# FFN: the raw turned tokens are put together by GpSimd, tile by tile, instead of by VectorE in two adds

## The reference, cut to what matters

```python
def rms_norm(x, g):
    y = xf * lax.rsqrt(jnp.mean(xf * xf, axis=-1, keepdims=True) + RMS_EPS)
    return (y * g).astype(x.dtype)

def swiglu(h, w_in, w_out):
    gate, up = jnp.split(h @ w_in, 2, axis=-1)
    return (jax.nn.silu(gate) * up) @ w_out

def macaron_half(x, g_pre, g_post, w_in, w_out):
    return x + FFN_RES_SCALE * rms_norm(swiglu(rms_norm(x, g_pre), w_in, w_out), g_post)
```

## Time and profile before

| | |
|---|---|
| median of 3 runs | 2520.59 us (2514.84 to 2521.19) |
| span of the profiled execution, first to last instruction | 2515.4 us |
| time of the profiled execution beside its span | not given |
| TensorE matmul busy | 2438.8 us, 97% |
| TensorE weight load busy | 2219.3 us, 88% |
| VectorE busy | 1502.0 us, 60% |
| ScalarE busy | 1078.2 us, 43% |
| GpSimd busy | 138.5 us, 6% |
| mean granted TensorE clock | 0.997 |

### The profile page before, as it was taken

How to read it: one execution, slowest core, us unless ns; L and a number is a source line. 1 busy time by engine, 2 the same in 40 slices (tenths; PEclk the granted TensorE clock), 3 DMA queues, 4 the chain that set the end, 5 groups by cost and what they waited for, 6 DMA issues and landing times. The chain is left out here.

```text
span 2515.4 us, 46249 instructions
## 1 busy us (share of the span) xinstructions
PE 2438.8 (97%) x18529; PEld 2219.3 (88%) x18529; DVE 1502.0 (60%) x2111; ACT 1078.2 (43%) x1873; POOL 138.5 (6%) x150
## 2 busy tenths in 40 slices
PE   8999999999988989999999999999999999999998
PEld 7998998899667877998999899899989779988997
DVE  7754764423546866873675687267462478735754
ACT  5542543322645654452353445245352444523542
POOL 0000001000203421000000100000010010000001
PEclk9999999999999999999999999999999999999999
DMA  4222324222480004322223332223423132322332
GB/s 134 84 86 74 84 65 152 60 75 62 151 267 20 4 13 142 85 75 88 80 84 124 119 84 75 96 73 90 136 75 97 63 102 84 92 80 75 90 105 104
DMA packets 285466, 229.41 MB, mean 91 GB/s; under 512 B 24924, under 2 KB 237046, under 8 KB 285320
## 3 DMA queue, kind: packets, MB, share of 16 engines
q1 hardware_dynamic: 285320, 227.38, 30.0%
HBM read 212.43 MB, written 14.91 MB: 90 GB/s over the span
## 5 line engine op out<-in xcount | busy, mean ns | idle before, releaser
L544 PE MATMUL ps<-row_hi,hid_hi 128*128 128x512 f32 x880 | 345.5, 393 | 0.0
L544 PE MATMUL ps<-row_hi,hid_lo 128*128 128x512 f32 x880 | 344.6, 392 | 0.0
L544 PE MATMUL ps<-row_lo,hid_hi 128*128 128x512 f32 x880 | 344.4, 391 | 0.0
L485 DVE TENSOR_TENSOR row_lo<-row_raw,row_hi 128x512 fp32r<-128x512 f32 x200 | 143.5, 731 | 265.9 <-ACT row_hi L477 265.7
L477 ACT ACTIVATE row_hi<-row_raw 128x512 fp32r<-128x512 f32 x200 | 124.1, 629 | 406.6 <-DMA row_raw<-in_ffn_w_out_dram 217.5
L544 PEld LDWEIGHTS ps<-row_lo,hid_hi 128*128 128x128 f32 x880 | 165.2, 188 | 36.9
L544 PEld LDWEIGHTS ps<-row_hi,hid_hi 128*128 128x128 f32 x880 | 165.1, 188 | 36.1
L544 PEld LDWEIGHTS ps<-row_hi,hid_lo 128*128 128x128 f32 x880 | 165.1, 188 | 36.0
L736 PE MATMUL ps<-t_hi,pair_hi 128*128 128x320 f32 x608 | 188.2, 310 | 3.0 <-DVE hid L1017 3.0
L736 PE MATMUL ps<-act_lo,pair_hi 128*128 128x320 f32 x608 | 187.9, 309 | 0.0
L736 PE MATMUL ps<-t_lo,pair_hi 128*128 128x320 f32 x608 | 187.9, 309 | 0.0
(11 more groups left out here) (453 smaller groups left out, 5688.9 us busy)
## 6 DMA issues: line engine op xcount, KB each, us to landing
pair_raw<-in_ffn_w_in_dram SPq DMA_DIRECT2D x104, 512.0 KB, 5.1
row_raw<-in_ffn_w_out_dram SPq DMA_DIRECT2D x160, 256.0 KB, 2.9
ring_raw<-in_ffn_w_in_dram SPq DMA_DIRECT2D x72, 512.0 KB, 5.2
pair_raw<-in_even_w_in_dram SPq DMA_DIRECT2D x22, 512.0 KB, 3.8
x_memory<-x SPq DMA_DIRECT2D x15, 512.0 KB, 2.6
x<-x_memory SPq DMA_DIRECT2D x15, 512.0 KB, 4.2
norm_buf<-in_norm_g_dram SPq DMA_DIRECT2D x12, 512.0 KB, 5.4
x<-in_x_prompt_dram SPq DMA_DIRECT2D x8, 512.0 KB, 4.9
```

The lines of the kernel that those rows point to most:

```text
L485: dve.tensor_tensor(row_lo[n][:, :], raw, row_hi[n][:, :].bitcast(F32), ALU.subtract).then_inc(s_row_lo, 1)
L544: mm = pe.matmul(ps[:, bank, :], a[:, k, t * P:(t + 1) * P], w[n][:, :], start=(k == 0 and w is row_hi and a is left_hi), stop=(k == kt - ...
```

## The change

- `dve_high_tokens` goes, with its two VectorE adds per FFN.
- `pool_tokens` is new. For each of the five tiles, GpSimd waits until `s_alo` shows that tile's low part, and adds `act_hi` and `act_lo` of that tile into `y`, 128x1024 per add. It is called for each FFN behind the GpSimd part of the norm that frees `y`; for the first FFN behind the constants.
- The order of `y` becomes tile first: five tiles, each with eight blocks of features of 128 tokens. `token_rows` follows.
- `dve_token_sums` is now called step by step (`dve_token_sum`). The first difference waits for all five adds of GpSimd (`s_tokens`). The counts of `s_tsum` go from five to four per FFN, also where ScalarE and `dve_token_low` wait for them.

```diff
         def token_rows(j):
-            return yflat.rearrange("p (k t a c) -> p k t a c", k=KD, a=2, c=P // 2)[:, 4 * j:4 * j + 4]
+            return yflat.rearrange("p (t k a c) -> p k t a c", k=KD, a=2, c=P // 2)[:, 4 * j:4 * j + 4]
...
-                act.wait_ge(s_tsum, 5 * f + i + 2)
+                act.wait_ge(s_tsum, 4 * f + i + 1)
...
-        def dve_high_tokens(dve, f):
-            raw = yflat.rearrange("p (k c) -> p k c", k=KD)
-            dve.wait_ge(s_alo, 5 * FFN_NORM[f] + TT)
-            for k in (0, 4):
-                dve.tensor_tensor(raw[:, k:k + 4, :], act_hi[:, k:k + 4, :].bitcast(F32),
-                                  act_lo[:, k:k + 4, :].bitcast(F32), ALU.add).then_inc(s_low_k if k == 0 else s_tsum, 1)
-
-        def dve_token_sums(dve, f):
+        def pool_tokens(pool, f):
+            m = FFN_NORM[f]
+            for t in range(TT):
+                cols = slice(t * P, (t + 1) * P)
+                pool.wait_ge(s_alo, 5 * m + t + 1)
+                pool.tensor_tensor(y[:, t, :].rearrange("p (k c) -> p k c", k=KD), act_hi[:, :, cols].bitcast(F32),
+                                   act_lo[:, :, cols].bitcast(F32), ALU.add).then_inc(s_tokens, 1)
+
+        def dve_token_sum(dve, f, i):
             b1, b2 = token_rows(0), token_rows(1)
...
+            if i == 0:
+                dve.wait_ge(s_tokens, TT * (f + 1))
+            else:
+                dve.wait_ge(s_tsum, 4 * f + i)
...
                 if c == 0:
-                    dve_high_tokens(dve, f)
                     tile(0, FFN_NORM[f])
-                    dve_token_sums(dve, f)
+                    for i in range(4):
+                        dve_token_sum(dve, f, i)
                     dve_token_low(dve, f, 0)
...
+            pool_tokens(pool, 0)
             pool_norm(pool, 1)
...
             pool_norm(pool, 2)
+            pool_tokens(pool, 1)
             pool_norm(pool, 3)
+            pool_tokens(pool, 2)
             pool_norm(pool, 4)
...
             pool_norm(pool, 5)
+            pool_tokens(pool, 3)
             pool_norm(pool, 6)
```

More of the change, by code:

```diff
@@ L391, in build @@
         s_prod, s_moved, s_joined = (sem(n) for n in ("sum_products", "products_moved", "products_joined"))
-        s_low_k, s_tsum, s_thi, s_tlo = (sem(n) for n in (
-            "tokens_low_k", "token_sums", "token_sums_hi", "token_sums_lo"))
+        s_tokens, s_tsum, s_thi, s_tlo = (sem(n) for n in (
+            "raw_tokens", "token_sums", "token_sums_hi", "token_sums_lo"))
         s_x_stored, s_x_again = sem("x_stored"), sem("x_loaded_again")
@@ L949, in dve_token_sums @@
-        def dve_token_sums(dve, f):
-            b1, b2 = token_rows(0), token_rows(1)
[L951 to L959, removed]
+        def pool_tokens(pool, f):
[5 more added lines that the diff above has]
+                                   act_lo[:, :, cols].bitcast(F32), ALU.add).then_inc(s_tokens, 1)
@@ new lines, in dve_token_sum @@
+        def dve_token_sum(dve, f, i):
+            b1, b2 = token_rows(0), token_rows(1)
+            if i == 0:
+                dve.wait_ge(s_tokens, TT * (f + 1))
+            else:
+                dve.wait_ge(s_tsum, 4 * f + i)
+            dst, left, right = ((b1[:, :, :, 0, :], b1[:, :, :, 1, :], b1[:, :, :, 0, :]),
+                                (b1[:, :, :, 1, :], b2[:, :, :, 1, :], b1[:, :, :, 1, :]),
+                                (b2[:, :, :, 1, :], b2[:, :, :, 1, :], b1[:, :, :, 0, :]),
+                                (b2[:, :, :, 0, :], b2[:, :, :, 0, :], b2[:, :, :, 1, :]))[i]
+            dve.tensor_tensor(dst, left, right, ALU.subtract).then_inc(s_tsum, 1)
@@ L963, in dve_token_low @@
             dve.wait_ge(s_thi, 4 * f + i + 1)
-            dve.wait_ge(s_tsum, 5 * f + 5)
+            dve.wait_ge(s_tsum, 4 * f + 4)
             dve.tensor_tensor(tiles_of(dst[1]), token_rows(j)[:, :, :, a, :], tiles_of(dst[0]).bitcast(F32),
```

## The result

The changed kernel takes 2534.49 us (median of 4 runs, 2531.22 to 2538.34) where the kernel before, on the same chip, takes 2519.41 (4 runs, 2514.84 to 2521.19): a ratio of 1.0061, 95% interval 1.0045 to 1.0077. It is 15.1 us slower. The forecast was 2538.0 within 2526 to 2545.

The account below looks back on a forecast made before the run. TensorE, busy 97% of the span, was taken to bound the kernel. Stalls of 10.1 us in three later FFNs and 2.5 in the first, plus 5.1 of clock falls, 17.7 us, on the 2520.59 median gave 2538.3 us; range 2526 to 2545.

Parts of the forecast that it names:

- the three small waits: TensorE's waits for the second weight pair's low part in the three later FFNs, 2.2 us in all, expected to vanish.
- the three instructions named: VectorE's scale L1170, gain L1208 and residual L1217 in the last tile's norm chain: single instances of 2 to 3.6 us.
- The adds' length: Each 128x1024 GpSimd add takes 2.38 us, between 1.89 and 2.6; the results are needed only after 7 us of slack.
- The holds: At each later FFN's head, GpSimd's first three adds hold VectorE's norm instructions 1.12, 0.60 and 2.38 us, 4.10 in sum.
- The part won back: TensorE's wait for the second pair's low part goes in each later FFN: 0.74 us won, leaving 3.36 us lost.
- The first FFN: The first two adds hold L448 by 0.53 and L1170 by 2.16 us; TensorE's turn is 2.5 us later, nothing won.
- The clock: Behind a 3.1 us TensorE idle piece in each later FFN, 3.4 us at half speed lose 1.7: 5.1 us.
- Edits at nothing: The tile-first order of `y`, GpSimd's queue, DMA and SyncE's waits were counted as costing nothing.
- Turns without weight: Rival: the adds fall where VectorE has slack, so only 2.2 us are won; 2518 us, chance 0.07.
- the freed time reaches TensorE: Rival: the 22 us taken off VectorE shorten the kernel in full; 2499 us, chance 0.03.
- Short adds: Rival: GpSimd's adds take 1.89 us each, stalls sum to 7.2 us and the clock stays; 2528 us, chance 0.10.
- the clock stays up: Rival: the same TensorE stalls but no fall to half speed, +12.6 us; 2533 us, chance 0.22.

Follow-up runs that it names:

- the run with the copies: Against the changed kernel, GpSimd copies each tile's high part into `y` instead of adding the low part; 2521.30 us, ratio 0.9998 to the kernel before.
- VectorE tile by tile: Against the changed kernel, VectorE makes the five per-tile adds in its idle gaps, GpSimd none; 2518.42 us (ratio 0.9988), on another chip 2519.88 (1.0000).
- adds in halves: Against the changed kernel, each GpSimd add is cut into two of 128x512; 2533.79 us, ratio 1.0048 to the kernel before.
- adds behind the last scaling: Against the changed kernel, GpSimd's first add waits until VectorE has scaled the norm's fifth tile; 2522.31 us, ratio 1.0007 to the kernel before.

## Why the prediction was right, and where its terms were off

**The mechanism held.** Work taken off VectorE didn't reach TensorE but for the three small waits; the turn-taking by whole instructions, read off rows of another norm and of a mixer, is what the heads show, at the three instructions named. The run without adds removes the loss, the run with the old adds in the new order too, and the two that only move adds move the loss with them. The Trainium skill ("GPSIMD Engine Reference", section 8) says that GpSimd contends with VectorE instructions of two SBUF inputs; the rows agree, and L1178, which reads one input from PSUM, passed. That a GpSimd instruction of one input holds VectorE too is what the run with the copies adds.

**The adds' length**: 2.38 us, from the line through the two shorter forms; measured 2.36 to 2.42 undisturbed. The figure of the Trainium skill ("GPSIMD Engine Reference", section 3.1), halved, had given 2.25: the measurement stands a little above it. Nothing waited for the results.

**The holds** were put at 1.12 + 0.60 + 2.38 = 4.10 us and measured 0.97 + 0.43 + 2.19 = 3.59. All three are 0.15 to 0.19 too large: VectorE's work starts about 0.15 us before GpSimd's row ends. At 2083.09 + 2.25 - 1.28 = 2084.06 it was at work, and the add's row runs until 2084.26. That same distance could have been read in the earlier trace rows: the subtraction at 972.53 had its 1.21 us of work from 973.64, GpSimd's product ended at 973.75.

**The part won back** was put at 0.74 and is 0.8 to 1.0 (the head without adds against before). A later FFN so costs 28.1 less 25.4 = 2.7 us and not 3.36: 8.1 and not 10.1 for three. This term was a fifth too large, by the two sizes above.

**The first FFN**: +2.5 us, with the same rule. TensorE's wait at the turn is 1.84 and 1.93 us in the two profiles of the change. The head grew by 2.3 in the second, and by 2.2 in two other kernels that keep these adds, but by 0.7 only in the first. There the turn's eight transposes took 1.09 us, the full-clock time, and not 1.97 or the 1.91 of the earlier trace rows: the clock had risen sooner. In the three others it was low for longer than before the change. Their transposes at full speed (1.03 or 1.04 us) come first at 23.6, 23.7 and 25.8 us, where before the change they come at 21.3; this is the later rise that I had set as a bound, and its cost lies inside their 2.2 to 2.3 us. The moment of the rise also moves where nothing is held: at the turn near 17.9 us the transposes took 1.10 us in one profile of VectorE tile by tile and 1.91 in the other, and the first heads are 22.82 and 23.69. Over the seven profiles without GpSimd's adds at this place the head is 22.8 to 23.1 us where they took 1.10 to 1.71, and 23.5 to 23.7 where they took 1.91. The kernel before, with 23.61, is one of the long ones, so the 0.7 us is too small a figure: beside the short ones it is 1.2 to 1.5. What sets the moment is open.

**The clock** was the term that was mis-sized: a fall at each later head, three times 1.7 = 5.1 us. Busy time per engine and PEclk around two turns of the changed kernel:

```profile
1012.02:1015.43 3.41, 1.10 (x9) 1.10 (x10) 2.58 (x3) 1.36 (x4) 0.00 (x0) 1.00 0.32 130
1015.43:1018.84 3.41, 3.41 (x12) 3.41 (x12) 1.23 (x1) 2.51 (x3) 3.35 (x2) 0.50 0.00 0
...
2096.20:2099.60 3.40, 0.63 (x5) 0.31 (x4) 1.82 (x4) 2.35 (x4) 0.00 (x0) 1.00 0.38 154
2099.60:2103.00 3.40, 3.40 (x24) 3.34 (x23) 2.03 (x2) 2.51 (x3) 2.51 (x2) 1.00 0.00 0
```

Behind the idle piece of 3.03 us the granted clock is 0.50, behind the one of 2.77 it is 1.00. Over the nine later heads of the three profiles that have such pieces (the change twice, the halves):

| kernel | FFN 1 | FFN 2 | FFN 3 |
|---|---|---|---|
| changed | 3.03, fell | 2.77, stayed | 2.77, stayed |
| changed, another chip | 3.01, fell | 2.77, fell | 2.77, stayed |
| adds in halves | 2.86, fell | 2.59, fell | 2.61, stayed |

Five of nine fell. A fall costs 1.5 to 1.6 us of head at FFN 2 (29.70 and 29.63 less 28.1) and 1.3 to 1.4 at FFN 1 (4.0 to 4.1 longer than before, less the 2.7), near the 1.7 predicted; the step that failed is "I count the fall each time". The predicted piece of 3.1 us was 2.8 in two of three heads because the holds were shorter, and at 2.6 to 2.8 us it goes either way. The argument from the earlier trace rows, that 2.55 us cost nothing at 984, rested on one execution and on fast transposes behind the piece. The first row is the same piece in the first profile of the change, the second its clock behind it, the third that of the profile before:

```profile
986.72 1.06 PE L1241 MATMUL ps<-ident,xn_buf 128*128 128x128 f32 x8 [2.55 <-DVE xn_buf L1171]
...
988.14:991.55 3.41, 3.41 (x10) 2.64 (x9) 0.72 (x2) 1.45 (x3) 0.00 (x0) 0.50 0.38 154
...
984.40:987.80 3.40, 3.34 (x19) 2.92 (x20) 2.02 (x4) 1.40 (x3) 0.00 (x0) 1.00 0.18 75
```

The transposes took their full-clock 1.06 us, and the fall came 1.4 us behind the piece. All ten other profiles have such a low stretch there, from 0.3 us before the end of the piece (once) to 1.4 us behind it, among them kernels whose heads have no stall. The profile before is the one of eleven without it. The Trainium skill ("TensorE: Matmul & The Clock Gate", Part 1) says of the start of a kernel that how many products run at the low clock changes from run to run; the rows show that at the first head (1.10 and 1.91 us of transposes at one turn), and the like in the middle of a kernel.

**The sum.** Predicted 17.7 us, measured 15.1 (and 15.0 on the second chip). By terms, in the two profiles of the change: the later heads 8.1 us instead of 10.1; the first 0.7 and 2.3 instead of 2.5; the falls at heads 1.4 and 2.9 instead of 5.1. That makes the 10.2 and 13.3 us of the table. The medians are 4.9 and 1.7 us more, and this part I hadn't in the sum; the falls that I counted too many made up for it. That the total came so near is in part luck. The missing part is no property of GpSimd's adds as far as the runs show: the median stands above the heads also where nothing stalls, by 2.7 us for the copies, 1.6 for no adds, 0.8 and 2.6 for VectorE tile by tile, 0.7 for VectorE's old adds in the new order (for the adds behind the last scaling it is 0.3 below).

The heads are measured against one profile of before, and that profile was a short one: its span of 2515.4 with the 1.7 us that the changed execution takes beside its span makes 2517.1, where the medians of before are 2519.4 to 2521.3. (Of the 5.2 us that the prediction had from the span to the median, 1.7 are then what an execution takes beside its span, and 3.5 are that this one was short.) Its shortness goes with the clock away from the heads. The profile of before has three stretches of 3.4 us at half speed there (one of 6.8 counts as two); six are in that of VectorE's adds in the new order, at an equal median, and six and seven in the two of the change. The part by which each profile's span exceeds 2515.4 us beyond its heads goes with that number, whatever the kernel: 2.0 us in the other profile with three, 0.7 with five, 3.6 and 4.5 with six, 5.4 to 6.9 with seven, 7.7 and 8.2 with eight, 10.6 with eleven. The 4.5 and 5.4 of the two profiles of the change are among these. What sets the number from one execution to the next is open.

**Edits at nothing** were nothing: the differences take 1.49 us in either order.

**Rivals.** "Turns without weight" and "the freed time reaches TensorE" fell with the first timeline. "Short adds" fell with 2.40. Of "the clock stays up" (2533) about half came true. The median lies between it and the forecast.

## What to carry to other kernels

Before work is moved from VectorE to GpSimd, look at what VectorE does while GpSimd's instruction would run: a two-input instruction in SBUF there stands still until it is over, and if it belongs to a chain that feeds the bounding engine, the saving on VectorE turns into a loss, here 15 us for 22 us taken off an engine that was 60% busy. Ask first what the removal can win at most (here 2.7 us of TensorE's waits, shown by leaving the work out), and fill the same engine's own idle pieces before another's. If GpSimd must do it, time its instructions behind the chain; cutting them smaller didn't help.

## What the runs showed of the hardware that was not expected

- A GpSimd copy with one input takes turns with VectorE as an add does: 1.97 us instead of 1.04, and VectorE's scaling 1.82 instead of 1.28. Small copies of 64x128 do too: 0.67 us instead of 0.29 behind a subtraction.
- VectorE's held instruction gets going 0.11 to 0.21 us before the end of the GpSimd row that holds it.
- GpSimd pays too: two adds side by side with VectorE's chain took 5.70 us instead of 4.80, five took 12.82 instead of 12.0.
- An idle piece of TensorE of 2.77 us was followed by half speed in one execution of the changed kernel and not in another, at the same place. One of 2.55 us had half speed beside it in ten of eleven profiles, and in some of them eight transposes ran at full speed in between.
